# Hybrid attention/mLSTM block with fast-product MLP: the seam before the MLP and its last two down groups rearranged

## What is computed

```
h   = rms_norm(x); p = h @ w_in                    # heads: window attention and mLSTM
mix = concat(rms_norm(att), rms_norm(mh))
x   = x + mix @ w_out                              # 1024 x 1024
h2  = rms_norm(x)
x   = x + (silu(h2 @ w_gate) * (h2 @ w_up)) @ w_down   # D_FF = 2816
```

## Time and profile before

| | |
|---|---|
| median of 3 runs | 1065.72 us (1064.81 to 1067.32) |
| the profiled execution's own time | 1066.38 us |
| its span in the trace | 1064.6 us, 13511 instructions |
| TensorE busy | 1034.7 us, 97% |
| VectorE, ScalarE, GpSimd busy | 682.1, 429.7, 707.4 us |

### The profile page before, as it was taken

One profiled execution on the slowest core, in us unless ns is written; L12 is line 12 of the kernel. 1 busy time (PEld: TensorE's weight loads), 2 busy tenths in 40 slices (PEclk: granted clock), 3 DMA queues, 4 the chain that ended last, 5 costly groups with the idle time before them and its releaser, 6 DMA issues.

```text
span 1064.6 us, 13511 instructions
## 1 busy us (share of the span) xinstructions
PE 1034.7 (97%) x4970; PEld 843.1 (79%) x4970; DVE 682.1 (64%) x790; ACT 429.7 (40%) x895; POOL 707.4 (66%) x555
## 2 busy tenths in 40 slices
PE   9999999998999997999999999999999999999987
PEld 7898877787878875888888888888888888888866
DVE  4259258767762578484857676575848576766386
ACT  7544133347740447433425143433334251434420
POOL 0138486716566237977878688687777786887873
PEclk9999999999999999999999999999999999999999
DMA  7123211130032001212121111111221111112104
GB/s 233 51 61 88 70 41 60 48 141 21 30 110 70 20 1 40 60 60 60 41 60 60 50 56 54 59 51 49 60 61 50 51 59 53 58 50 60 60 20 158
DMA packets 71162, 66.06 MB, mean 62 GB/s; under 512 B 5305, under 2 KB 53689, under 8 KB 71097
## 3 DMA queue, kind: packets, MB, share of 16 engines
q1 hardware_dynamic: 70104, 64.71, 19.6%
q10 hardware_dynamic: 992, 0.49, 0.2%
HBM read 60.48 MB, written 4.21 MB: 61 GB/s over the span
## 4 chain that ended last, share of the span: by engine, by line
PE 85%; DVE 5%; ACT 4%; issue 2%; POOL 2%; DMA 1%; SPq 0%; POOLq 0%; DVEq 0%; ACTq 0%
PE banks L738 27%; PE banks L739 26%; PE banks L740 26%; ACT prob L1367 1%; PE banks L827 1%; PE banks L824 1%; PE banks L758 1%; DMA w_raw<-in_w_in 1%; DVE prob L1804 1%; POOL wr_lo L677 1%; DVE smx L1809 1%; PE banks L915 1%; DVE hf_raw L1536 0%; PE banks L803 0%; DVE h2buf L1554 0%
## 5 line engine op out<-in xcount | busy, mean ns | idle before, releaser
L677 POOL TENSOR_TENSOR wr_lo<-wr_raw,wr_hi 128x512 fp32r<-128x512 f32 x231 | 315.2, 1394 | 47.8 <-ACT wr_hi L1197 42.7
L671 POOL TENSOR_TENSOR wr_raw<-wr_raw,wr_raw 128x512 f32<-128x512 f32 x132 | 191.2, 1459 | 126.5 <-DMA wr_raw<-in_w_gate 45.5
L738 PE MATMUL banks<-hf_hi,wr_hi 128*128 128x512 f32 x616 | 244.0, 396 | 7.1 <-issue 5.8
L739 PE MATMUL banks<-hf_lo,wr_hi 128*128 128x512 f32 x616 | 243.4, 395 | 0.0
L740 PE MATMUL banks<-hf_hi,wr_lo 128*128 128x512 f32 x616 | 243.3, 395 | 0.0
L1959 DVE TENSOR_TENSOR x<-banks,x 128x1024 f32<-128x1024 f32 x154 | 188.1, 1223 | 60.3 <-PE banks L740 54.4
L1197 ACT ACTIVATE wr_hi<-wr_raw 128x512 fp32r<-128x512 f32 x231 | 134.7, 624 | 144.1 <-POOL wr_raw L671 141.9
L738 PE MATMUL banks<-w_hi,actT_hi 128*128 128x512 f32 (+1 forms) x448 | 172.1, 384 | 2.4 <-DVE x L1768 1.5
L740 PE MATMUL banks<-w_hi,actT_lo 128*128 128x512 f32 (+1 forms) x448 | 168.2, 375 | 0.0
L739 PE MATMUL banks<-w_lo,actT_hi 128*128 128x512 f32 (+1 forms) x448 | 167.8, 375 | 0.0
L738 PEld LDWEIGHTS banks<-hf_hi,wr_hi 128*128 128x128 f32 x616 | 116.3, 189 | 36.2 <-issue 6.5
(11 more groups left out here) (201 smaller groups left out, 1246.9 us busy)
## 6 DMA issues: line engine op xcount, KB each, us to landing
wr_raw<-in_w_up SPq DMA_DIRECT2D x46, 256.0 KB, 2.9
wr_raw<-in_w_gate SPq DMA_DIRECT2D x44, 256.0 KB, 2.9
wr_raw<-in_w_down SPq DMA_DIRECT2D x44, 256.0 KB, 2.6
w_raw<-in_w_in SPq DMA_DIRECT2D x32, 256.0 KB, 3.5
w_raw<-in_w_out SPq DMA_DIRECT2D x16, 256.0 KB, 2.7
x<-in_x SPq DMA_DIRECT2D x8, 512.0 KB, 6.4
out<-x SPq DMA_DIRECT2D x16, 256.0 KB, 2.2
x_in<-in_x SPq DMA_DIRECT2D x7, 512.0 KB, 4.6
```

Source lines behind the costliest of these rows:

```text
L671: nc.gpsimd.tensor_tensor(wr_raw[slot(q, f)][:, :], wr_raw[slot(q, a)][:, :], wr_raw[slot(q, b)][:, :], ALU.subtract).then_inc(wsum, 1)
L677: nc.gpsimd.tensor_tensor(wr_lo[s][:, :], wr_raw[s][:, :], wr_hi[s][:, :].bitcast(F32), ALU.subtract).then_inc(wf_lo, 1)
L738: nc.tensor.matmul(ps, x_hi, wh, start=first, stop=False, skip_group_check=more)
L739: nc.tensor.matmul(ps, x_hi, wl, start=False, stop=False, skip_group_check=more)
```

## The change

Five things are done:

1. Units 8, 10, 12 and 14 of the output projection use banks 4 and 5 in place of 0 and 1 (`acc`), and a part waits for the additions of the unit two before.
2. VectorE makes the fourth sum and the low part of form 3; GpSimd's `fourth_sum` and its low part are gone. VectorE makes the low parts of forms 5 and 6 in halves. The high parts in `EARLY_HIGH` stand earlier.
3. In the seam form 5 goes ahead of form 6 in both quads (`SEAM`), (1,2) goes to bank 0, and what ScalarE and VectorE do is reordered to suit.
4. The last two down quads are one group (`last_downs`): for each form and pair of tiles the matmuls of both are accumulated in the same banks, and VectorE adds once for both, so 14 additions (the last split in two of 512 columns) take the place of 28. Quad 32 has seven slots of its own, freed by products of the last up quad.
5. For that group, GpSimd's and ScalarE's work is in orders written out by hand (`LAST_SUMS`, `LAST_HIGH`, `LAST_LOW`), and the low parts of the last activation forms are VectorE's, spread over `dve_up`, `act_sums` and `dve_last`.

The number of matmuls stays the same.

```diff
         for i, at in enumerate([Z + 2 * SIDE + SLOT * i for i in range(6)]
-                               + [R0, M1 + SIDE, M1 + SIDE + SLOT, V]):
+                               + [R0, M1 + SIDE, M1 + SIDE + SLOT, V]
+                               + [W1 + 3 * SIDE + SLOT, M0 + 2 * SIDE, M0 + 2 * SIDE + SLOT, Z, Z + SLOT,
+                                  M0 + 3 * SIDE, M0 + 3 * SIDE + SLOT]):
...
-        EARLY_HIGH = ([], [(0, 1)], [(0, 2)], [(0, 6)], [(0, 5)], [(0, 7), (0, 3)], [(0, 4), (1, 1)], [(1, 2)])
+        EARLY_HIGH = ([(0, 1), (0, 2)], [(0, 6), (0, 5)], [(0, 7), (0, 3)], [(0, 4)], [], [(1, 1)], [(1, 2)], [])
+        SEAM = (1, 2, 5, 6, 7, 3, 4)
...
+        LAST_SUMS = [(0, 5), (0, 6), (1, 5), (0, 7), (0, 4), (1, 6), (1, 4), (1, 7)]
+        LAST_HIGH = [(0, 1), (0, 2), (1, 1), (0, 6), (1, 2), (0, 5), (0, 7), (0, 3), (0, 4),
+                     (1, 6), (1, 5), (1, 7), (1, 3), (1, 4)]
+        LAST_LOW = [(0, 1), (1, 1), (0, 2), (0, 6), (1, 2), (1, 6), (0, 5), (1, 5), (0, 7), (1, 7),
+                    (0, 3), (1, 3), (0, 4), (1, 4)]
...
         def slot(q, f):
 
+            if q == NQ - 1:
+                return WR + at_form(f)
             return (7 * q + at_form(f)) % WR
...
+        def acc(j):
+
+            return 4 if j >= T and j % 2 == 0 else 0
...
+            if q == NQ - 1:
+                after = 2 if slot(q, f) == WR else 6 if slot(q, f) < WR + 5 else 5
+                engine.wait_ge(gu_done, 7 * GU["up", JS - 1] + at_form(after) + 1)
+                return
...
-            def fourth_sum(t):
-
-                a = slice(t % 4 * P, (t % 4 + 1) * P)
-                pool.wait_ge(h2_raw, 8)
-                pool.wait_ge(h2_sum, 3 * (t - 3))
-                nc.gpsimd.tensor_tensor(hf_raw[3][:, :, a], hf_raw[3][:, :, a], hf_raw[6][:, :, a],
-                                        ALU.subtract).then_inc(h2_s4, 1)
...
+            for q in range(NR):
                 n = 16 * (q // 2 + 1)
...
-                    fourth_sum(4)
-                    fourth_sum(5)
...
                     pool.wait_ge(b11_again, 16)
                     pool.wait_ge(b12_s[q % 2], n)
                     block_sum(q, 5, 7, 5)
...
+            last_low(0, 1)
+            last_sum(0, 6)
+            last_sum(1, 5)
+            last_low(1, 1)
+            last_sum(0, 7)
+            last_sum(0, 4)
+            last_low(0, 2)
+            last_low(0, 6)
+            last_sum(1, 6)
+            last_sum(1, 4)
+            last_low(1, 2)
+            last_sum(1, 7)
+            pool.wait_ge(wsum, sum_count(NQ - 1, 7))
+            last_low(1, 6)
+            for f in FORMS[3:]:
+                last_low(0, f)
+                last_low(1, f)
...
                         pe.wait_ge(acc_free[part], UNITS // 2)
+                    elif j == T:
+                        pe.wait_ge(s_evac, T)
                     else:
-                        pe.wait_ge((wa_free, x1_ready)[part], j)
+                        pe.wait_ge((wa_free, x1_ready)[part], j if j < T else j - 1)
...
+                        last = three(bank[acc(j) + part][:, :], actT_hi[:, t // 4, k, a], actT_lo[:, t // 4, k, a],
...
                 pe.wait_ge(h2_split, T)
+                pe.wait_ge(x1_ready, 2 * T - 1)
                 half_product(gate, 0, 1, True)
                 half_product(up, 1, 1, True, T - 1)
                 half_product(e, 0, 2, True)
-                half_product(f_, 1, 2, True)
+                pe.wait_ge(wa_free, 2 * T)
+                half_product(bank[0][:, :], 1, 2, True)
+                pe.wait_ge(h2_flo, 2)
+                half_product(f_, 0, 5, True)
                 pe.wait_ge(copied, copy_of(0, 0))
-                pe.wait_ge(h2_flo, 2)
+                pe.wait_ge(h2_flo, 4)
                 half_product(gate, 0, 6, False)
-                pe.wait_ge(added, add_of(1, 0))
-                pe.wait_ge(h2_flo, 3)
-                half_product(f_, 0, 5, True)
                 pe.wait_ge(copied, copy_of(0, 1))
-                pe.wait_ge(h2_flo, 4)
+                pe.wait_ge(h2_flo, 5)
                 half_product(gate, 0, 7, False)
                 pe.wait_ge(copied, copy_of(0, 2))
-                pe.wait_ge(h2_flo3, 1)
+                pe.wait_ge(h2_flo, 6)
                 half_product(f_, 0, 3, False)
                 pe.wait_ge(added, add_of(0, 1))
-                pe.wait_ge(h2_flo, 5)
+                pe.wait_ge(h2_flo, 7)
                 half_product(gate, 0, 4, False)
+                pe.wait_ge(added, add_of(0, 2))
+                half_product(f_, 1, 5, True)
                 pe.wait_ge(copied, copy_of(1, 0))
                 half_product(up, 1, 6, False)
-                pe.wait_ge(added, add_of(0, 2))
-                half_product(f_, 1, 5, True)
...
+            def last_downs():
+
+                base, top = 14 * (JS - 2), 7 * (JS - 2)
+                for n, f in enumerate(FORMS):
+                    first = {1: 0, 6: 0, 7: 0, 4: 0}.get(f, 4)
+                    opens = f in (1, 2, 5)
+                    for h in range(2):
+                        if n != 1:
+                            pe.wait_ge(down_add, base + (2 * n - 3 if n >= 2 else -1) + h)
+                        elif h == 0:
+                            pe.wait_ge(added, 3 * len(GU))
+                            pe.wait_ge(silu_done, 4 * JS)
+                        else:
+                            pe.wait_ge(act_raw, 8 * (JS - 1) + 4)
+                        for i, j in enumerate(LAST):
+                            q = NR + i
+                            pe.wait_ge(wf_lo, low_count(q, f))
+                            pe.wait_ge(act_lo_s, 7 * j + n + 1)
+                            s = slot(q, f)
+                            for t in (2 * h, 2 * h + 1):
+                                a = slice(t * P, (t + 1) * P)
+                                last = three(bank[first + t][:, :], af_hi[i][f][:, a], af_lo[i][f][:, a],
+                                             wr_hi[s][:, :], wr_lo[s][:, :], opens and i == 0, True,
+                                             not (opens and i == 0))
+                                if i == 1 and n == 6 and t == 2:
+                                    last.then_inc(dn_done, 1)
+                        last.then_inc(dn_done, 1)
...
             def act_first():
+                early, late_ = slice(0, 2 * P), slice(2 * P, 4 * P)
                 copy_product(sg[1], bank[4], product(0, 1))
+                act.wait_ge(wb_done, 2 * T)
+                act.wait_ge(h2_sum, 5)
+                form_high(5, early)
+                act.wait_ge(h2_sum, 7)
+                form_high(6, early)
                 form_tile(T - 1)
-                act.wait_ge(wb_done, 2 * T)
-                act.wait_ge(h2_sum, 9)
-                form_high(6, slice(0, 3 * P))
                 copy_product(af_raw[0][1], bank[7], product(1, 1))
-                act.wait_ge(h2_sum, 12)
-                form_high(6, slice(3 * P, 4 * P))
-                form_high(5, slice(0, 4 * P))
+                act.wait_ge(h2_sum, 13)
+                form_high(5, late_)
+                act.wait_ge(h2_sum, 15)
+                form_high(6, late_)
                 form_high(7, slice(0, 4 * P))
-                act.wait_ge(h2_s4, 4)
+                act.wait_ge(h2_sum, 16)
                 form_high(3, slice(0, 4 * P))
                 act.wait_ge(h2_raw, 2 * T)
+                copy_product(sg[4], bank[6], product(0, 5))
+                form_high(4, slice(0, 4 * P))
                 copy_product(sg[2], bank[4], product(0, 6))
...
+            def act_last():
+                j = JS - 1
+                act_high(j, 1)
+                weight_high(NR + 1, 1)
+                weight_high(NR, 6)
+                weight_high(NR + 1, 2)
+                weight_high(NR, 5)
+                act_high(j, 2)
+                weight_high(NR, 7)
+                weight_high(NR, 3)
+                weight_high(NR, 4)
+                act_high(j, 6)
+                weight_high(NR + 1, 6)
+                act_high(j, 5)
+                weight_high(NR + 1, 5)
+                act_high(j, 7)
+                weight_high(NR + 1, 7)
+                act_high(j, 3)
+                weight_high(NR + 1, 3)
+                act_high(j, 4)
+                weight_high(NR + 1, 4)
...
+                dve.wait_ge(h2_sum, n + 3)
+                if t == T - 1:
+                    form_low(5, slice(2 * P, 4 * P), 3)
+                combine(3, 3, 6, ALU.subtract)
...
                 gated(j, b, 7, bank[7])
+                if last:
+                    act_low(j, 2)
...
                 gated(j, b, 4, af_raw[b][4])
+                if j == JS - 1:
+                    act_low(j, 1)
...
             def dve_first():
+                early, late_ = slice(0, 2 * P), slice(2 * P, 4 * P)
+                dve.wait_ge(h2_sum, 12)
+                form_low(5, early, 1)
                 form_tile(T - 1)
-                dve.wait_ge(h2_sum, 12)
-                dve.wait_ge(h2_s4, 3)
```

(37 more changed lines are left out.)

134 lines of the change are left out of this document (78 added, 56 removed).

## The result

The changed kernel takes 1059.28 us (median of 4 runs, 1058.61 to 1060.01); the kernel before, beside it, took 1066.36 (1064.81 to 1067.32). The ratio is 0.9944, 95% interval 0.9929 to 0.9959: faster by 0.4 to 0.7%. The prediction was 1052.2 with a range of 1048 to 1057: right in sign, outside the range, and the gain is half of the 13.5 us forecast.

The account below looks back on a forecast made before the run. TensorE, busy 97% of the span, was taken to bound the kernel, leaving its idle and half-clock time to win. From 1065.72 us, 6.2 at the seam and 7.3 at the end (13.5) gave 1052.2, range 1048 to 1057.

Parts of the forecast that it names:

- The seam (6.2 us): Up to the second gate quad: its start moves from 447.8 to 441.6 us, a gain of 6.2 us.
- VectorE's turn: Output projection's last units: VectorE's loop of additions, scale and sums, 8.5 us a turn, sets when the last transposes start.
- Rival (b): Seam: moved work gives nothing since VectorE and GpSimd exclude each other; seam gain 1.5 us, median 1056.9; chance 0.13.
- The fall in the seam (2.2 us): Behind the 2.8 us wait before the last transposes the clock falls to half, costing 2.2 us.
- The 550 us between them have no gap to win: Between the seam and the end, the two edited places: TensorE has no idle time there to win.
- each instruction of one adds its price to the other if they meet: VectorE sums of two SBUF tiles and GpSimd instructions exclude each other: 0.60 or 2.20 us on VectorE, 1.25 or 4.5 on GpSimd.
- The wait before form 2 (1.7 to 1.9 us): Last group, second half of form 2: TensorE waits 1.7 to 1.9 us for GpSimd, late with its queued instructions.
- rival (d): End: loads of down 10 land late, each us going into the wait before form 2; 3 us give 1055.2; chance 0.12.
- The end in all (7.3 us): Last two down quads and tail: 6.5 us up to the last matmul plus 0.8 in the tail, 7.3 us.
- The two copy waits (0.9 each): Seam, form 6 directly followed by form 7 in one bank: TensorE waits 0.9 us for ScalarE's copy, twice, 1.9.
- Rival (a): Seam and end: the clock stays up; 1048.8 us at both places, 1050.5 at one; chance 0.3.
- Rival (c): Seam, 402 to 442 us: half clock does not end, price 30 us, 1080 in all, slower; chance 0.03.

Follow-up runs that it names:

- seam_only: The changed kernel's seam (parts 1 to 3) with the end of the kernel before, down 9 and down 10 as two quads; 1064.35 us, ratio 0.9990.
- end_fill_gap: Changed kernel, with GpSimd's sums (0,7) and (0,4) moved ahead of the first sum of down 10; 1053.37 us, ratio 0.9886.
- e1_add_ahead: Changed kernel, but in the second gate quad VectorE adds the fifth product's bank after three of its six low parts; 1056.32 us, ratio 0.9920.
- end_low_12: Changed kernel, with only GpSimd's low part (1,2) moved ahead of (0,6) at the end; 1055.92 us, ratio 0.9912.
- hold_pool: Changed kernel, but GpSimd starts down 0's weights only after VectorE added the second gate quad's fifth product; 1055.66 us, ratio 0.9905.
- e2_end_order: Changed kernel, with GpSimd's sums needing no new load ahead of down 10's first sum, and low part (1,2) ahead of (0,6); 1053.17 us, ratio 0.9887.
- e3_low_early: Changed kernel, but ScalarE makes the high parts of (1,1) and (1,2) in unit 12, not units 13 and 14; 1056.12 us, ratio 0.9906.
- end_only: The old seam of the kernel before with the changed kernel's end (parts 4 and 5); 1060.93 us, ratio 0.9967.
- banks_only: Kernel before with part 1 alone: units 8, 10, 12 and 14 in banks 4 and 5, with their waits; ratio 0.9982.
- all_three: Changed kernel with the earlier addition in the second gate quad, GpSimd's other order at the end, and the early high parts; 1046.99 us, ratio 0.9832.

## Why the prediction failed, point by point

- **Where the 13.5 us went.** In the profiled execution 6.5 us are missing: 4.3 in the stretch behind the seam, 1.6 at the end and 0.6 in the seam.
- **The seam (6.2 us): right in its size and its places.** Gating 7 is 5.6 us earlier, though TensorE came to the first transposes 0.85 us later than before (356.84 against 355.99), and seam_only has 6.5. The single wait before the transposes was forecast at 2.8 us and is 2.85, the fall behind it happened, and none of VectorE's low parts was waited for. VectorE's turn is 8.26 us, forecast 8.2 (a slip in the sum, 3.03 for half of 6.14, moves nothing). Rival (b) as told, low parts waited for after (1,2), did not happen in the seam.
- **The fall in the seam (2.2 us): mis-sized, and made good by luck.** From the last transposes to gating 7 it is 39.36 us with the fall (changed) and 39.09 without it (end_fill_gap), so in all the fall cost 0.3 us. Without it the sum would have been 37.3 to the second gate quad, and end_fill_gap needed 38.9: small waits such as the 0.41 and 0.26 and strides of 0.232 us were not in it. The two errors cancel. Where the clock stayed down longer (e1_add_ahead and end_low_12), the stretch is 40.6 us.
- **"The 550 us between them have no gap to win": the step that failed.** It was true that there was no gap to win. I took it to mean that there was nothing to lose, looked at 500 to 600 us only, and let the account of the seam end where the second gate quad starts. There VectorE had one addition of a bank behind six low parts, with nearly nothing to spare: TensorE did not stand still for it in the trace of before, and a chain 3.1 us longer gave a wait of 2.75 and a fall. It cost 4.3 us, and in e1_add_ahead and hold_pool, where that wait is gone, the stretch is 3.3 and 3.4 us shorter. The price that made it longer was in my own text ("each instruction of one adds its price to the other if they meet"); I applied it to the seam and the end, but not to the quad that follows. GpSimd's low parts come later against VectorE because (1,6) now stands one product later and its slot comes free later; the two load rows above show that, though no kernel here puts (1,6) back alone.
- **The wait before form 2 (1.7 to 1.9 us): right mechanism, a mis-sized term.** It is 3.36 us. The sum had the loads of down 10 land near 1003.4 and five of twelve instructions done by 1007.1, with down 9 starting at 1011.44. Down 9 started 1.3 us earlier, so by its start these are 1002.1 and 1005.8. In the trace the load landed near 1005.5, the fourth instruction, the sum (1,5), starts only at 1005.59, after 2.29 us of idle time, and the fifth is done at 1008.57, 2.8 us late. The other seven took 11.9 us in place of the 12.95 forecast, which leaves the last 1.7 us late. This is rival (d), which had 0.12, though not each us of lateness went into the wait as it said: 3.4 us of the load became 1.7. end_fill_gap shows it. The clock fell behind it, as taken.
- **The end in all (7.3 us):** 5.7 came (4.5 in the group, 1.2 in the tail; the tail was forecast at 0.8). What is missing is the mis-sized wait, 1.6 us, and 0.3 us of the fall behind it: of the 5.3 us that the group loses against e2_end_order, 3.36 are the wait, which leaves 1.9 where 1.6 was taken.
- **The two copy waits (0.9 each):** 0.69 each. The additions cost nothing at the end, as said.
- **Rival (a)** did not come: the clock fell at both places. Its 8 us for a seam without a fall would have been too much: end_fill_gap has 7.0. **Rival (c)** neither: it was back at 1.00 each time.
- **The range** left out a second loss behind the seam because no case had a place for it. (b) at 1056.9 and (d) at 1055.2 would have covered the time only together, and I had put their mixture at 0.02.

## What to carry to other kernels

Where an edit shifts two engines that slow each other against one another, follow the queues past the edited place to the first stretch that is the same in both kernels, and ask there how much each consumer has to spare: an unbroken row of nines says that nothing is idle, not that nothing is tight. In an in-order queue, put what the bound engine waits for ahead of what is wanted a quad later, and give an engine that waits for loads the work that needs none. What a fall of the clock costs depends on what stands behind it. The wait in the second gate quad cost 3.0 us without a fall (e3_low_early, 566.45 against 563.44) and 4.3 with one (changed, 567.78). The fall in the seam cost 0.3 us, since without it two other waits stood there.

## What the runs showed of the hardware

- **The same wait can leave the clock up or not.** The wait of 2.84 or 2.85 us before the last transposes stands in the traces of eight kernels; in seven the windows behind it show 0.50, in end_fill_gap 1.00. The wait of 2.75 to 2.77 us in the second gate quad stands in six; the clock fell in three (changed, seam_only, end_low_12) and stayed at 1.00 in three (e3_low_early, e2_end_order, end_fill_gap). The e2_end_order trace has one of each:

```profile
402.00:404.00 2.00, 2.00 (x9) 1.97 (x10) 1.93 (x4) 2.00 (x3) 0.00 (x0) 0.50 0.00 0
462.00:464.00 2.00, 2.00 (x10) 1.60 (x9) 0.00 (x0) 1.59 (x4) 2.00 (x3) 1.00 0.00 0
```

  The two waits in attention, 1.94 to 1.95 us near 243 and 1.87 to 1.91 near 313, stand in all these traces, and in each the clock fell at exactly one of them: at the first in four (end_only, banks_only, end_fill_gap, end_low_12), at the second in the others, among them. Behind waits of 0.69, 0.85 and 0.87 us the clock was 1.00. In the prediction a fall was either taken or not; a term with a chance would have been closer.
- **The price of a meeting:** six low parts of VectorE took 3.69 us alone, 8.09 with GpSimd for most of the time, and 9.66 beside it throughout, 0.6 and 1.6 us each. The prediction's prices gave 1.85 for one that meets GpSimd.
- **Loads issued close together land late:** of the loads of down 10, three issued at 999.59, 1000.07 and 1000.54 in the changed kernel landed after 3.2, 4.4 and 4.9 us, where the median of these 256 KB loads is 2.6.
- **Gate quads in the steady stretch now and then have a wait of 0.9 us** for the same kind of addition, in some executions (two in end_only and in banks_only, one in e1_add_ahead, end_fill_gap and end_low_12, none in all_three). I have no cause for when.
